# Two-block decoder kernel: four token-major projections stream 512 weight columns per stationary tile instead of 256, and one of them runs in one piece

## The reference, cut to what matters

```python
# first block
h = rmsnorm(x, mix_pre_norm); u = h @ w_in            # conv inputs, q, k, v, g of a retention
y = concat([conformer_conv(...), retention_group(hq, hk, hv, hg)]) @ w_out
x = x + rmsnorm(y, mix_post_norm)
h = rmsnorm(x, ffn_pre_norm)
x = x + rmsnorm((silu(h @ w_ffn_gate) * (h @ w_ffn_up)) @ w_ffn_down, ffn_post_norm)
x = x + rmsnorm(sigmoid(x @ w_ple_gate) * (p @ w_ple_proj), ple_post_norm)
# second block
h = rmsnorm_2(x, norm_mix)
(hq, hi, hff, hfb, hg, nq, nk, nv, cq, gates...) = split_cols(h @ w_in_2)
y_hg = hgrn2_branch(hq, hi, hff, hfb, hg, ...)         # gated linear attention; values are hi
y_na = neighbourhood_attention(nq, nk, nv, ...)        # values are nv
y_ca = memory_cross_attention(cq, mem_n, w_kv, w_o)    # mem_n @ w_kv gives memk and memv
x = x + (sum of sigmoid(gate) * y) @ w_out_2
x = x + conv_ffn(rmsnorm_2(x, norm_ffn)); return rmsnorm_2(x, norm_final)
```

## Time and profile before

| | |
|---|---|
| time, three runs | 1084.84, 1082.06, 1082.46 us; median 1082.46 us |
| span of the profiled execution, first to last instruction | 1082.2 us |
| time of the profiled execution itself | not listed apart; its span lies 0.26 us below the median of the three runs |
| PE busy | 997.5 us (92% of the span) |
| DVE, ACT, POOL busy | 666.2, 507.4, 465.6 us |
| chain that ended last | PE 75%, DVE 20%, ACT 2% |

### The profile page before, as it was taken

How to read it: one execution, slowest core, us unless ns; L and a number is a source line. 1 busy time by engine, 2 the same in 40 slices (tenths; PEclk the granted TensorE clock), 3 DMA queues, 4 the chain that set the end, 5 groups by cost and what they waited for, 6 DMA issues and landing times.

```text
span 1082.2 us, 18278 instructions
## 1 busy us (share of the span) xinstructions
PE 997.5 (92%) x7768; PEld 967.7 (89%) x7768; DVE 666.2 (62%) x862; ACT 507.4 (47%) x738; POOL 465.6 (43%) x195
## 2 busy tenths in 40 slices
PE   6979079999999998989989999999999989999996
PEld 6979068999999997979989999898899989999996
DVE  4599986466666314466568896984545456566422
ACT  5444034454444444545543454545445346666531
POOL 2759110243443443314654553373577324434441
PEclk8989689999999999999989999999999999999999
DMA  7435201455455553315533333534245424555541
GB/s 292 173 117 195 78 1 42 153 205 184 171 190 191 175 180 117 117 47 187 196 120 115 117 137 92 182 117 139 98 154 193 156 103 174 193 188 170 189 156 39
DMA packets 29153, 158.15 MB, mean 146 GB/s; under 512 B 8945, under 2 KB 9345, under 8 KB 10640
## 3 DMA queue, kind: packets, MB, share of 16 engines
q1 hardware_dynamic: 29008, 156.91, 40.7%
q0 software_dynamic: 64, 0.08, 0.0%
HBM read 155.87 MB, written 1.12 MB: 145 GB/s over the span
## 4 chain that ended last, share of the span: by engine, by line
PE 75%; DVE 20%; ACT 2%; issue 1%; DMA 1%; SPq 0%; POOL 0%; DVEq 0%; ACTq 0%
PE pj L1310 64%; DVE conv_y L917 8%; PE sc L1477 3%; PE pj L1326 2%; PE st L1353 2%; DVE sq L859 1%; PE sc L1567 1%; DVE x L875 1%; DVE rstd L827 1%; DVE y L872 1%; DMA raw<-wstream 1%; ACT w_hi L509 1%; PE sc L1536 1%; DVE rstd_h L827 1%; DVE ret_inv L970 1%
## 5 line engine op out<-in xcount | busy, mean ns | idle before, releaser
L467 POOL TENSOR_TENSOR w_lo<-raw,w_hi 128x1024 fp32r<-128x1024 f32 x179 | 448.8, 2512 | 584.4 <-ACT w_hi L509 584.2
L1310 PE MATMUL pj<-h,w_hi 128*128 128x256 f32 x2816 | 515.8, 286 | 14.3 <-DVE h L851 8.9
L509 ACT CAST w_hi<-raw 128x1024 fp32r<-128x1024 f32 x284 | 296.9, 1048 | 411.2 <-PE pj L1310 369.8
L1310 PEld LDWEIGHTS pj<-h,w_hi 128*128 128x128 f32 x2816 | 442.1, 193 | 20.1 <-issue 15.5
L1310 PE MATMUL pj<-h,w_lo 128*128 128x256 f32 x1408 | 399.9, 284 | 0.0
L1310 PEld LDWEIGHTS pj<-h,w_lo 128*128 128x128 f32 x1408 | 271.7, 193 | 0.0
L837 DVE TENSOR_TENSOR w_lo<-raw,w_hi 128x1024 fp32r<-128x1024 f32 x105 | 136.8, 1303 | 148.9 <-ACT w_hi L509 148.1
L1310 PE MATMUL pj<-ff,w_hi 128*128 128x256 f32 x704 | 125.9, 282 | 0.0
L1310 PEld LDWEIGHTS pj<-ff,w_hi 128*128 128x128 f32 x704 | 108.2, 188 | 0.1
L1310 PE MATMUL pj<-ff,w_lo 128*128 128x256 f32 x352 | 99.0, 281 | 0.0
L917 DVE SCALAR_TENSOR_TENSOR conv_y<-conv_in,vec,conv_y 128x256 f32<-128x256 f32 x120 | 91.1, 833 | 0.0
(11 more groups left out here) (226 smaller groups left out, 1324.3 us busy)
## 6 DMA issues: line engine op xcount, KB each, us to landing
raw<-wstream SPq DMA_DIRECT2D x142, 1024.0 KB, 4.9
toep_t<-toep SPq DMA_DIRECT2D x16, 96.0 KB, 3.4
x<-xt SPq DMA_DIRECT2D x2, 512.0 KB, 5.0
y<-memt SPq DMA_DIRECT2D x1, 1024.0 KB, 11.2
w_ple<-wproj SPq DMA_DIRECT2D x1, 1024.0 KB, 7.4
out_t<-y SPq DMA_DIRECT2D x4, 256.0 KB, 2.1
decay<-decay_tab SPq DMA_DIRECT2D x1, 768.0 KB, 7.2
con<-consts SPq DMA_DIRECT2D x1, 448.0 KB, 6.4
```

The costliest lines, as they stand in the source:

```text
L467: nc.gpsimd.tensor_tensor(w_lo[:, u % UNITS], unit_of_raw(u), as_f32(w_hi[:, u % UNITS]), ALU.subtract).then_inc(lo_ready["pool"], 1)
L509: nc.scalar.copy(w_hi[:, u % UNITS], unit_of_raw(u)).then_inc(hi_ready, 1)
L1310: last = mm(dst, w[a], src[:, b, kt], start=kt == 0 and i == 0, stop=kt == kts - 1 and i == 2)
```

## The change

The four token-major stages become `token_quad` fills of 32 blocks (four units). v, memv and nv are one fill each instead of two, hi is two instead of four. In a quad the two token tiles have one PSUM bank each, the loop over the eight feature tiles is outermost, and every matmul streams 512 columns. There are still three banks, so a quad takes two turns of them (`FIRST_BANK`). ACT empties the two banks with one copy each. The host lays out the weight blocks of these stages in groups of four column blocks instead of two.

memv now stands in one piece ahead of the `ffn_pre` statistic. On DVE, the call that split units on behalf of memv 0 stood ahead of the `ffn_pre` norm; now the call there is for wout 3, whose units are split already, and the one for memv stands behind the norm. The places of the levels among the side fills are renumbered.

```diff
-    ("conv", 4, 16, "dve"), ("qk", 4, 16, "act"), ("v", 2, 16, "act"), ("g", 2, 16, "act"),
-    ("memk", 2, 16, "act"), ("wout", 4, 16, "act"), ("memv", 2, 16, "act"),
+    ("conv", 4, 16, "dve"), ("qk", 4, 16, "act"), ("v", 1, 32, "act"), ("g", 2, 16, "act"),
+    ("memk", 2, 16, "act"), ("wout", 4, 16, "act"), ("memv", 1, 32, "act"),
...
-        LEVEL_AFTER = {1: 0, 3: 1, 5: 2, 7: 3, 9: 4, 11: 5, 12: 6}
-        DIAGONAL_AFTER, CROSS_AFTER = 1, 13
+        LEVEL_AFTER = {0: 0, 1: 1, 3: 2, 5: 3, 7: 4, 9: 5, 10: 6}
+        DIAGONAL_AFTER, CROSS_AFTER = 0, 11
...
+            def token_copy(name, j, dst):
+
+                wait_fill(name, j)
+                nc.scalar.copy(dst[:, 0], bank(name, j)[:].rearrange("p a s -> p (a s)"))
+                nc.scalar.copy(dst[:, 1], bank(name, j, 1)[:].rearrange("p a s -> p (a s)")
+                               ).then_inc(freed["act"], 1)
...
             squares_of_x("mix_post")
-            copy_fill("memv", 0, mem_v[:, :, 0:256])
+            token_copy("memv", 0, mem_v)
             root("ffn_pre")
             hi_of_h("ffn_pre")
-            copy_fill("memv", 1, mem_v[:, :, 256:512])
...
             post_norm("mix_post", "mix_post")
+            feed_behind("wout", 3)
+            norm_to_h("ffn_pre", "ffn_pre")
             feed_behind("memv", 0)
-            norm_to_h("ffn_pre", "ffn_pre")
-            feed_behind("memv", 1)
...
+            def token_quad(name, j, src, ready=None):
+
+                open_fill(name, j)
+                for kt in range(KT):
+                    w = take(4)
+                    if ready is not None:
+                        ready(kt)
+                    for tt in range(2):
+                        dst = bank(name, j, tt)[:].rearrange("p a s -> p (a s)")
                         for i, (wa, xa) in enumerate(PASSES):
+                            last = mm(dst, src[:, xa, kt, tt * P:tt * P + P], w[wa],
                                       start=kt == 0 and i == 0, stop=kt == KT - 1 and i == 2)
+                    step(last, at_block[0])
...
-            token_pair("memv", 0, mem_n)
+            token_quad("memv", 0, mem_n)
             norm_stat("ffn_pre", 4)
-            token_pair("memv", 1, mem_n)
```

More of the change, by code:

```diff
@@ L68, with bank_owner @@
 TOKEN_STAGES = ("v", "memv", "hi", "nv")
+FIRST_BANK = [sum(1 + (f[0] in TOKEN_STAGES) for f in FILLS[:n]) for n in range(len(FILLS) + 1)]
+def bank_owner(turn):
+    return next(n for n in range(len(FILLS)) if FIRST_BANK[n] <= turn < FIRST_BANK[n + 1])
 _ENDS = sorted({FIRST_BLOCK[n + 1] for n in range(len(FILLS))} | {UB * (u + 1) for u in range(NUNITS)})
@@ L604, in _ @@
                 copy_fill("qk", 2 + j, k_raw[:, 2 * j:2 * j + 2])
-            for j in range(2):
-                copy_fill("v", j, v_ret[:, :, 256 * j:256 * j + 256])
+            token_copy("v", 0, v_ret)
             for j in range(2):
@@ L1285, in take @@
                     pe.wait_ge(lo_ready[LO_ENGINE[u]], lo_count(u, LO_ENGINE[u]))
-                if count == 1:
-                    return [w[:, u % UNITS, b % UB] for w in (w_hi, w_lo)]
                 return [w[:, u % UNITS, b % UB:b % UB + count].rearrange("p a b -> p (a b)") for w in (w_hi, w_lo)]
@@ L1296, in open_fill @@
                 n = fi(name, j)
-                if n >= PJ:
-                    who = FILLS[n - PJ][3]
-                    pe.wait_ge(freed[who], freed_count(n - PJ, who))
+                for turn in range(FIRST_BANK[n], FIRST_BANK[n + 1]):
+                    if turn >= PJ:
+                        owner = bank_owner(turn - PJ)
+                        pe.wait_ge(freed[FILLS[owner][3]], freed_count(owner, FILLS[owner][3]))
                 assert at_block[0] == FIRST_BLOCK[n]
-                return pj[n % PJ]
+                return bank(name, j)
             def tile_out(dst, src, kts=KT, ready=None):
@@ L1374, in _ @@
                 pair("qk", j, h)
-            for j in range(2):
-                token_pair("v", j, h)
+            token_quad("v", 0, h)
             for j in range(2):
@@ L1609, in blocks, with token_blocks @@
         return [[w[kt * P:(kt + 1) * P, m * P:(m + 1) * P] for kt in range(k)] for m in cols]
-    def token_blocks(w, pairs):
+    def token_blocks(w, quads):
         k = w.shape[0] // P
-        return [[w[kt * P:(kt + 1) * P, m * P:(m + 1) * P] for kt in range(k) for m in (2 * q, 2 * q + 1)]
-                for q in pairs]
+        return [[w[kt * P:(kt + 1) * P, m * P:(m + 1) * P] for kt in range(k) for m in range(4 * q, 4 * q + 4)]
+                for q in quads]
     def vecs(a, tiles):
@@ L1630, in host_layout @@
         add(a[j], a[4 + j])
-    add(*a[8:16], *token_blocks(w_in, (8, 9)), *a[20:24])
+    add(*a[8:16], *token_blocks(w_in, (4,)), *a[20:24])
     w_kv = g["w_mem_kv_2"][0]
@@ L1643, in host_layout @@
     b = blocks(w_in2, range(80))
-    add(*b[16:32], *b[0:8], *token_blocks(w_in2, range(4, 8)), *b[32:40], *b[40:48],
-        *token_blocks(w_in2, (24, 25)), *b[52:56])
+    add(*b[16:32], *b[0:8], *token_blocks(w_in2, (2, 3)), *b[32:40], *b[40:48],
+        *token_blocks(w_in2, (12,)), *b[52:56])
     for base, w in ((56, g["w_hg_o_2"][0]), (72, g["w_ca_o_2"][0]), (64, g["w_na_o_2"][0])):
```

27 lines of the change are left out of this document (9 added, 18 removed).

## The result

| | median of the runs | ratio to before, 95% interval |
|---|---|---|
| before | 1083.26 us (1082.06 to 1084.84, 4 runs) | |
| changed | 1096.49 us (1095.46 to 1097.96, 4 runs) | 1.0121 [1.0104, 1.0138] |

The change makes the kernel slower by 13.2 us. The forecast was 8.2 us slower, with a range that ended at 1095; the direction was right and the size was not. So the profiled execution of before, with a span of 1082.2, was near 1084 and not at the median, as the prediction had it. That is why the spans differ by 13.9 us and the medians by 13.2.

The account below looks back on a forecast made before the run. The prediction took PE's matmul stream, busy 92% of the span, as the bound, with DVE's chain in places. Terms 0 + 6.0 + 2.0 + 0.2 gave +8.2 us on 1082.5, so 1090.7 us, range 1087 to 1095.

Parts of the forecast that it names:

- I take 215.6 ns for a 512-column matmul: All token stages: a quad of 48 matmuls takes 10.35 us instead of 11.50; five quads take 5.75 us off PE.
- The upper bound of 240: Pace of a 512-column matmul: at most 240 ns, twice 119.8, which would mean no gain.
- v, 0: Stage v: PE finishes 1.15 us earlier and waits that much longer for k_raw; 0 us.
- memv's order, +6.0: memv to ff: later root, h and unit 40's split make ff 0 end later; +6.0 us.
- memv's clock, +2.0: ff 0 after PE's standstill: granted clock falls to half; +2.0 us, between 0 and 3.
- hi 1: -1.3: Second hi quad: earlier rounding and key copy let level 1 start 1.27 us earlier, kept to level 5.
- nv, cross and cq: +1.5 at first: Level 5 to first softmax: level 6, cross and normalisation come later; +0.2 us net of hi 1's gain.
- The clock falls again in mhg 0: Rival at mhg 0: the clock drops again where PE stands some 2.3 us; +2.6, 1093.3 us, chance 0.14.
- no pace gain at 512 columns: Rival for all quads: 512-column matmuls run no faster per column; 1093.1 us, chance 0.06.

Follow-up runs that it names:

- kernel 15: The kernel before with v alone as a quad: 1083.46 us over 12 runs, ratio 1.0001.
- Kernel 5: The kernel before, no quads, with memv's two 256-column fills both ahead of the ffn_pre statistic and the late split: 1090.68 us, ratio 1.0068.
- kernel 6: The kernel before with memv as one quad ahead of the statistic, but DVE splits units 40 and 42 before the norm: 1086.28 us, ratio 1.0029.
- kernel 2: The kernel before with memv alone as in the change, units fed behind the norm: 1089.24 us, ratio 1.0058.
- kernel 1: The changed kernel with memv alone as it was before; v, hi and nv stay quads: 1089.88 us, ratio 1.006.
- kernel 3: The kernel before with hi alone as two quads: 1083.16 us over 10 runs, ratio 1.0000.
- kernel 8: v, hi, nv as quads, memv as before, plus eight POOL splits held until DVE has finished the level it grows: 1080.84 us, ratio 0.9979.
- Kernel 14: The kernel before with nv alone as in the change, plus POOL held back at units 166, 167, 170 and 171: 1084.08 us, ratio 1.0011.
- kernel 4: The kernel before with nv alone as one quad, level 6 behind it and cq 0 ahead of cross: 1087.6 us, ratio 1.0044.
- kernel 9: The changed kernel with eight POOL splits held until DVE has finished the level it grows: 1090.18 us, ratio 1.007.
- kernel 7: The kernel before with memv as one quad, cut at feature tile 4 around the ffn_pre statistic, units fed as before: 1083.46 us, ratio 1.0000.

## Why the prediction was wrong, step by step

- **"I take 215.6 ns for a 512-column matmul": failed.** The quads took 11.19 us (memv) and 10.89 us (nv) for 48 matmuls, 233 and 227 ns each. The 13 ns beyond the columns that the 256-column matmul has (119.8 against 107) are paid again by each 512-column matmul (213 + 14 to 20). The step read the pace from f32 operands that aren't rounded, whose records follow each other without them. It was a reading across kinds of operand. A quad saves 0.3 to 0.6 us, not 1.15, and PE's busy time fell by 1.1 us. The upper bound of 240 held. memv's quad is 0.8 us longer than the sum has it (11.19 - 10.35), of which 0.6 reach the root, and nv's is 0.5 longer, so this step alone doesn't make the miss.
- **The pace in the Trainium skill** ("TensorE: Matmul & The Clock Gate", Back-to-back issue gap): neither its 131 ns for sustained streams nor its 216 ns for isolated matmuls is what rounded f32 operands show here.
- **v, 0: right**, by kernel 15. The wait for k_raw grew by 2.1 us and not by 1.15. Most of the rest is a wait of 1.23 us for POOL's w_lo that PE had at the start of v before (at 81.33 us) and has no more.
- **memv's order, +6.0: right in mechanism, small by 0.65.** ff 0 started 6.65 us later. The root came 3.1 us later and not 2.5, since it hung on the statistic behind the slower quad. Kernel 5 shows that order alone makes it, kernel 6 that the late split of unit 40 is about half.
- **memv's clock, +2.0: too high.** From ff 0 to the first statistic of the next norm there are 1320 matmuls in 159.85 us. Before, the same stretch is 381.16 - 222.79 = 158.37. The clock cost 1.5 us. The sizes of the two terms err in opposite ways, so that memv's 8.1 us in the trace against 8.0 in the sum is partly luck. Repeated runs put all of memv at +6.3 (kernel 2) and +6.6 (changed kernel less kernel 1), so 8.0 was too much by about 1.5.
- **"hi 1: -1.3": failed, and with it the sum.** This is the step that the overshoot comes from, together with what the nv step left out. It reads the end of `grow` from before, "ready at 581.7", as if it would stay. In the same rows one instruction of 3.43 us already stood among others of 1.2, and the prediction didn't ask what made it long, though it names the same stall in the normalisation. In the changed kernel a second one came: +1.0 us from level 0 to level 1 (593.99 - 575.31 = 18.68 against 17.65), and 1.5 us more for the slow clock in level 1. In kernels 1 and 3 the later start is there and the slow clock isn't. With POOL held back the -1.2 appears (kernel 8).
- **"nv, cross and cq: +1.5 at first": right as far as the order goes.** Kernel 14 has +1.6 in its trace and +1.1 in its time. What it left out are the collisions in `grow(5)` and `grow(6)`, worth 2.3 us, or 2.8 with the slow clock of kernel 4. The prediction knew of the stall ("0.69 us alone and 2.36 where POOL was splitting") and counted it in the normalisation only. There it was right: DVE's chain from its first long reciprocal to its end takes 21.57 us against 22.75, -1.2 where -1.1 was forecast.
- **The rival "The clock falls again in mhg 0": not in the changed kernel's trace.** The 48 matmuls from 719.60, behind the waits of 2.23 and 0.87 us, take 5.74 us, 120 ns each. But the clock did fall at level 1, behind a wait of 2.48 us; and in kernels 1, 4 and 9 it fell in mhg 0 too (0.57, 0.51 and 0.60 in the first 2 to 3 us behind the same wait), where it cost 0.4 us in kernel 4 and not 2.6.
- **The rival "no pace gain at 512 columns", 1093.1:** nearer to the measured pace, still short by 3.4 us, because the missing term is not the pace.

The delay of 15.3 us at the first softmax, taken apart by the traces: 8.1 up to the diagonal (8.0 in the sum), 0.8 in the diagonal and behind it (0, and within its scatter), 1.0 up to level 1 (-1.3), 1.5 in level 1 (0), 3.9 from level 3 to the softmax (+1.5). The misses are 2.3 at hi 1, 1.5 at the clock behind it and 2.4 at nv; the collisions stand behind the first and the last, and made the wait of 2.48 us that the clock fell behind. Kernels 1 and 3 had the same wait without the slow clock, so that part came by chance.

The parts measured alone add up to 6.3 + 0.0 + 4.8 + 0.1 = 11.2 us, and the whole is 13.2. Each has an interval of about 1 to 1.6 us to either side, so this may be chance. The slow clock in level 1 doesn't explain it: kernel 1, which has no memv, is already 1.6 us above its parts (6.5 against 4.9), and its level 1 takes 4.14 us at full clock. In its trace the clock fell at another place, behind the 2.01 us of waiting at `cross`. Window, length, PE busy, clock, DMA share, GB/s:

```profile
674.70:680.00 5.30, 5.30 (x33) 0.68 0.33 75
```

From `cross` to DVE's first step of the normalisation it is 683.10 - 674.69 = 8.41 us there, and 680.30 - 673.52 = 6.78 in kernel 4 at full clock, 1.6 less. So slow stretches came behind waits that the change adds, but not behind each of them and not in every trace. How often each comes in an execution wasn't measured.

## What to carry to other kernels

A change on one engine moves the times at which buffers come free, and with them the work of engines that the change doesn't touch. Where a DVE chain is on the path, look in the trace for instructions of one kind with two durations, ask what POOL does at that moment, and ask where POOL's work will be after the change. A wait that holds POOL back until the chain is over cost nothing here, where POOL had slack (the longest wait of PE for a split of POOL is 5.2 us with and without gates), and took 8.8 us off kernel 1. A root or split that sits behind a long fill is better kept in the middle of it: kernel 7 cuts a long accumulation halfway through its loop, keeps the 512-column stream, and turns +6.3 us into 0.0.
